# Told keys in three parts, x1 turned ahead of a fold piece, row places by when they come free, two more weight heads kept, 16-row bands

## The reference, cut to what matters

```python
def _peer_block(xb, wq, sub_keys, u_tab, v_tab):
    q = (xb @ wq).reshape(T, PEER_HEADS, 2, PEER_HALF)
    s = jnp.einsum('thpd,hpkd->thpk', q, sub_keys).astype(jnp.float32)
    s1, i1 = lax.top_k(s[:, :, 0], PEER_TOPK)          # 16 of 128
    s2, i2 = lax.top_k(s[:, :, 1], PEER_TOPK)
    cand = (s1[..., :, None] + s2[..., None, :]).reshape(T, PEER_HEADS, PEER_TOPK * PEER_TOPK)
    cidx = (i1[..., :, None] * PEER_KEYS + i2[..., None, :]).reshape(T, PEER_HEADS, PEER_TOPK * PEER_TOPK)
    top, sel = lax.top_k(cand, PEER_TOPK)              # 16 of 256
    idx = jnp.take_along_axis(cidx, sel, axis=-1)
    gate = jax.nn.softmax(top, axis=-1)
    h = jax.nn.gelu(jnp.einsum('td,thkd->thk', xb, u_tab[idx]).astype(jnp.float32), approximate=False)
    return jnp.einsum('thk,thkd->td', (gate * h).astype(xb.dtype), v_tab[idx])
# the pool mixer, per group g with window w in (2, 4, 8, 16): d = (mean of the last w rows of u) - u
```

## Time and profile before

| | |
|---|---|
| median of 3 runs | 3123.96 us |
| the profiled execution's own time | 3122.1 us |
| its span, first to last instruction | 3120.0 us |
| mean granted TensorE clock | 0.866 |
| busy: TensorE, VectorE, ScalarE, GpSimd | 74%, 71%, 31%, 43% |
| moved by the DMA engines | 1258.71 MB, mean 403 GB/s |

### The profile page before, as it was taken

One profiled execution on the slowest core, in us unless ns is written; L12 is line 12 of the kernel. 1 busy time (PEld: TensorE's weight loads), 2 busy tenths in 40 slices (PEclk: granted clock), 3 DMA queues, 4 the chain that ended last, 5 costly groups with the idle time before them and its releaser, 6 DMA issues.

```text
span 3120.0 us, 53529 instructions
## 1 busy us (share of the span) xinstructions
PE 2321.9 (74%) x21008; PEld 929.5 (30%) x21008; DVE 2219.2 (71%) x5418; ACT 954.4 (31%) x2437; POOL 1330.2 (43%) x1143
## 2 busy tenths in 40 slices
PE   8989998578777787668776667576677576767656
PEld 4633333233333333224432122122222122222112
DVE  1476777678878879656677666587777777777775
ACT  1422332334435435112322222132332332223222
POOL 1034344334444343345655544344444444444443
PEclk9999999889889899777878888798888898789867
DMA  7699999999999999999999999999999999999997
GB/s 282 238 420 421 420 402 419 417 419 384 419 418 409 418 409 404 415 406 418 416 418 412 417 413 398 418 414 420 409 415 403 420 419 421 402 420 419 420 416 309
DMA packets 201412, 1258.71 MB, mean 403 GB/s; under 512 B 24001, under 2 KB 27609, under 8 KB 60225
## 3 DMA queue, kind: packets, MB, share of 16 engines
q0 software_dynamic: 159808, 1133.76, 88.2%
q1 hardware_dynamic: 39916, 121.25, 10.0%
q10 hardware_dynamic: 1436, 0.29, 0.0%
HBM read 1226.74 MB, written 28.65 MB: 402 GB/s over the span
## 4 chain that ended last, share of the span: by engine, by line
DMA 31%; PE 14%; DVE 6%; POOL 4%; issue 3%; DVEq 2%; ACT 2%; POOLq 0%; ACTq 0%
DMA ring<-in_uv,idx 31%; PE sc L1044 7%; DVE ring L1929 3%; POOL ring L2151 3%; PE sc L1077 2%; PE route L1019 2%; DVEq L1939 1%; PE sc L1046 1%; ACT diag L1451 1%; POOL front L2167 1%; PE sc L943 0%; ACT hgelu L1446 0%; PE work L1065 0%; PE sc L913 0%; DVE x L1978 0%
## 5 line engine op out<-in xcount | busy, mean ns | idle before, releaser
L2151 POOL DMA_INDIRECT ring<-in_uv,idx x1056 | 1250.1, 1184 | 1617.5 <-PE sc L1046 1396.0
L1929 DVE CUSTOM_DVE_ANT_0 ring<-ring,xn_cur 128x1024 f32<-128x1024 f32 x1056 | 1280.8, 1222 | 649.2 <-DMA ring<-in_uv,idx 645.2
L1044 PE MATMUL sc<-ring,diag 32*32 32x512 f32 x8192 | 1229.1, 719 | 676.7 <-ACT diag L1451 631.6
L1046 PE MATMUL sc<-ring,diag 32*32 32x512 f32 x8192 | 1229.0, 719 | 0.0
L1044 PEld LDWEIGHTS sc<-ring,diag 32*32 32x32 f32 x8192 | 270.5, 117 | 1449.1 <-ACT diag L1451 1039.1
L1446 ACT ACTIVATE hgelu<-hdot 128x2 f32<-128x2 f32 x528 | 107.5, 204 | 1858.8 <-DVE hdot L1929 1857.9
L1451 ACT ACTIVATE diag<-gate_d,hgelu 128x32 f32<-128x32 f32 x1056 | 281.8, 314 | 21.2
L1046 PEld LDWEIGHTS sc<-ring,diag 32*32 32x32 f32 x8192 | 269.8, 117 | 1.9 <-issue 1.7
L589 PE MATMUL sc<-big,front 128*128 128x512 f32 x384 | 177.8, 606 | 2.2 <-DVE front L1558 2.1
L1446 ACT ACT_TABLE_LOAD x129 | 165.5, 1283 | 2.3
L1019 PE MATMUL route<-big,xnT 128*128 128x256 f32 x560 | 135.7, 397 | 0.0
(11 more groups left out here) (314 smaller groups left out, 2337.6 us busy)
## 6 DMA issues: line engine op xcount, KB each, us to landing
front<-wqk_scratch SPq DMA_DIRECT2D x21, 1024.0 KB, 13.0
ring<-in_uv,idx POOLq DMA_INDIRECT x1056
big<-in_w_in SPq DMA_DIRECT2D x8, 1024.0 KB, 13.8
wqk_scratch<-front SPq DMA_DIRECT2D x8, 1024.0 KB, 6.3
big<-wqk_scratch SPq DMA_DIRECT2D x8, 1024.0 KB, 22.2
x<-x_scratch SPq DMA_DIRECT2D x12, 512.0 KB, 9.0
ring<-in_wq_t POOLq DMA_DIRECT2D x10, 512.0 KB, 14.0
front<-in_x SPq DMA_DIRECT2D x8, 512.0 KB, 6.9
```

The lines of the kernel that those rows point to most:

```text
L1044: pe.matmul(sc[own, 0, :], diag[own, r, :], uv_rows[own, place, D:D + W4], start=opens_sum, stop=closes).then_inc(row_added[r], 1)
L1046: pe.matmul(sc[other, 1, :], diag[own, r, :], uv_rows[own, place, D + W4:2 * D], start=opens_sum, stop=closes).then_inc(row_added[r], 1)
L1929: dve.tensor_tensor_reduce(uv_rows[:, row_of(k), 0:D], uv_rows[:, row_of(k), 0:D], xn_cur[:, :], 1.0, 0.0, ALU.mult, ALU.add, hdot[:, n % ...
L2151: pool.indirect_dma_start(uv_rows[:, row_of(k), :], None, uv, bass.IndirectOffsetOnAxis(ap=idx[:, n % PH, j:j + 1], axis=0)).then_inc(row_ ...
```

## The change

First choice of keys (`choose_first`, `tell_keys`): for n = 0 alone, the index of the best expert is written as soon as the best 8 of each half are known, that of the next 7 after the best 8 sums, that of the last 8 after all; `fetch` waits for each part by itself. x1 of the first tile is turned before fold piece 14, which moves with piece 15 behind all four output products of tile 1; piece 14 comes to lie in `x2`, so that place 7 is free of it, and it is loaded two pieces earlier. The ring's places are taken in the order 5, 6, 7, 2, 3, 0, 1, 4. The product of the pooled half for both column halves of tile 1 now stands ahead of the heads' half. Heads 4 and 3 stay from n = 27 on: `STREAMED` is 27, the eight loads into `big` are reordered and four of them stand at slots 181, 182, 184 and 185, right behind the reads of the keys and values that they overwrite. Of u of the tile before and of its band only the last 16 rows are loaded and multiplied.

```diff
+BEFORE = PAD + 1
-STREAMED = 29
+STREAMED = 27
+STAYING = (4, 3, 2, 1, 0, 5, 6, 7)
 def fold_slot(j):
-    return -LEAD + (1, 2, 3, 4, 5, 6, 7, 8, 9, 10, 11, 12, 12, 13, 13, 15)[j]
+    return -LEAD + (1, 2, 3, 4, 5, 6, 7, 8, 9, 10, 11, 12, 12, 13, 16, 16)[j]
+def stay_slot(i):
+    if i < 2:
+        return ATT[-1].scores[H - 1][-1] + 1 + i
+    if i < H:
+        return ATT[-1].values[H - 1] - 1 + i
+    return BACK_FREE + i - H
 def pooled_slot(t, c):
-    return (POOLED_0[c], a.out[c])[t] if t < EARLY else a.norm[c]
+    return (POOLED_0[c], a.out[0])[t] if t < EARLY else a.norm[c]
-        FIRST_ROW = 5
+        ROWS = (5, 6, 7, 2, 3, 0, 1, 4)
-            return (k + FIRST_ROW) % RING
+            return ROWS[k % RING]
-            return (turned, other, xt[0], xt[1], xn_cur[:, :], turned, other, xn_cur[:, :])[j - PH]
+            return (turned, other, xt[0], xt[1], xn_cur[:, :], turned, x2[:, :], xn_cur[:, :])[j - PH]
-        WQ_AFTER = {12: 7, 13: 8, 14: 9, 15: 12}
+        WQ_AFTER = {12: 7, 13: 8, 15: 12}
+        FIRST_KEYS = (0, 1, TOPK // 2)
             def band(t):
-                        mm = pe.matmul(bank[w][:, cols], a.up[:, cols], a.bp[:, cols], start=False, stop=True)
+                        rows = slice(0, T if t < EARLY else BEFORE)
+                        mm = pe.matmul(bank[w][:, cols], a.up[rows, cols], a.bp[rows, cols], start=False, stop=True)
...
                 elif n < STREAMED:
                     pe.wait_ge(wst_in[head_of(n) % 2], 16 * streamed_to(n))
                 else:
-                    pe.wait_ge(wqk_in, 16 * PH)
+                    for h in range(COPIES * (n - N0), COPIES * (n - N0 + 1)) if n >= N0 else (head_of(n),):
+                        pe.wait_ge(big_in[STAYING.index(h)], 16 * 2)
...
-                if s == ROUTE_0 - 2:
-                    norm_root(0)
                 for j in range(FOLDS):
                     if s == fold_slot(j):
                         keep_fold(j)
+                        if j == FOLDS - 5:
+                            norm_root(0)
...
+            def tell_keys(at, told):
+                P = at.stop - at.start
+                over = lambda ap: ap.unsqueeze(1).to_broadcast([T, P, TOPK])
+                place = [cand[:, s * T:s * T + P * TOPK].rearrange("p (i j) -> p i j", i=P) for s in range(2)]
+                dve.drain()
+                dve.tensor_scalar(ab[:, 0, at], ind2[:, at], 4, None, ALU.logical_shift_right)
+                dve.tensor_scalar(ab[:, 1, at], ind2[:, at], 15, None, ALU.bitwise_and)
+                dve.drain()
+                dve.tensor_copy(abf[:, :, at], ab[:, :, at])
+                dve.drain()
+                for s in range(2):
+                    dve.tensor_tensor(place[s], abf[:, s, at].unsqueeze(2).to_broadcast([T, P, TOPK]), over(iota[:, :]),
+                                      ALU.is_equal)
+                dve.drain()
+                for s in range(2):
+                    dve.tensor_tensor(place[s], place[s], over(ind1f[:, s, :]), ALU.mult)
+                dve.drain()
+                for s in range(2):
+                    dve.tensor_reduce(pick[:, s, at], place[s], AX.X, ALU.add)
+                dve.drain()
+                dve.scalar_tensor_tensor(out=idx[:, 0, told], in0=pick[:, 0, told], scalar=float(NK),
+                                         in1=pick[:, 1, told], op0=ALU.mult, op1=ALU.add).then_inc(idx_ready, 1)
+            def choose_first():
+                take_scores(0)
+                first_keys(0)
+                dve.drain()
+                dve.tensor_copy(ind1f[:, :, 0:8], ind1[:, :, 0:8])
+                dve.drain()
+                dve.scalar_tensor_tensor(out=idx[:, 0, 0:1], in0=ind1f[:, 0, 0:1], scalar=float(NK),
+                                         in1=ind1f[:, 1, 0:1], op0=ALU.mult, op1=ALU.add).then_inc(idx_ready, 1)
+                other_keys(0)
+                first_pairs(0)
+                dve.tensor_copy(ind1f[:, :, 8:16], ind1[:, :, 8:16])
+                tell_keys(slice(0, 8), slice(1, 8))
+                dve.drain()
+                dve.max(top2[:, 8:16], cand_lo[:, :])
+                dve.tensor_scalar(gst[:, NTOP:NTOP + 1], top2[:, 0:1], -1.0, None, ALU.mult).then_inc(top_ready, 1)
+                dve.drain()
+                dve.max_index(ind2[:, 8:16], top2[:, 8:16], cand_lo[:, :])
+                tell_keys(slice(8, 16), slice(8, 16))
...
             def fetch(n, j):
                 k = n * TOPK + j
-                if j == 0:
-                    pool.wait_ge(idx_ready, n + 1)
-                if k == RING - FIRST_ROW:
+                if n == 0 and j in FIRST_KEYS:
+                    pool.wait_ge(idx_ready, FIRST_KEYS.index(j) + 1)
+                if n >= 1 and j == 0:
+                    pool.wait_ge(idx_ready, n + len(FIRST_KEYS))
+                if k == ROWS.index(2):
+                    pool.wait_ge(ready[S0], filled(S0, ("out", EARLY - 1, 0)))
+                if k == ROWS.index(0):
                     pool.wait_ge(ready[S1], filled(S1, ("out", EARLY - 1, 1)))
...
-                sp.dma_start(a.up, u_d[tile_rows(t - 1), :]).then_inc(att_in, 16)
+                sp.dma_start(a.up[0:BEFORE, :], u_d[t * T - BEFORE:t * T, :]).then_inc(att_in, 16)
...
-                sp.dma_start(by_group(a.bp), c_band_prev).then_inc(band_in, 16)
+                sp.dma_start(by_group(a.bp)[0:BEFORE], c_band_prev[T - BEFORE:T]).then_inc(band_in, 16)
...
-                for h in range(PH):
-                    if s == BACK_FREE + h:
-                        sp.wait_ge(ready[S1], filled(S1, ("out", NT - 1, 1)))
-                        sp.dma_start(wqk_sb[:, h, :], wqk_d[h]).then_inc(wqk_in, 16)
+                for i, h in enumerate(STAYING):
+                    if s == stay_slot(i):
+                        if i < 2:
+                            sp.wait_ge(ready[S1], filled(S1, ("scores", NT - 1, H - 1, 1)))
+                        elif i < H:
+                            sp.wait_ge(ready[WK], filled(WK, ("values", NT - 1)))
+                        else:
+                            sp.wait_ge(ready[S1], filled(S1, ("out", NT - 1, 1)))
+                        sp.dma_start(wqk_sb[:, i, :], wqk_d[h]).then_inc(big_in[i], 16)
```

More of the change, by code:

```diff
@@ L443, in front_and_experts @@
         stage_out = [sem(f"stage_out{i}") for i in range(2)]
-        w_in_in = [sem(f"w_in_in{k}") for k in range(KD)]
+        big_in = [sem(f"big_in{k}") for k in range(KD)]
         w_out_in = [sem(f"w_out_in_{n}") for n in ("heads", "pooled")]
@@ L486, in front_and_experts @@
         wst_in = [sem(f"wst_in{i}") for i in range(2)]
-        wqk_in = sem("wqk_in")
         gate_w_in = sem("gate_w_in")
@@ L570, in project_early @@
                 for k in range(KD):
-                    pe.wait_ge(w_in_in[k], 16)
+                    pe.wait_ge(big_in[k], 16)
                     for t in range(EARLY):
@@ L761, in front_step @@
                             out_pooled(t, c)
+                    for c in range(2):
                         if s == a.out[c]:
@@ L1011, in route @@
                             mm = pe.matmul(bank[RT][tokens, 0:256], xnT[:, k, tokens],
-                                           wqk_sb[:, head, k * 256:(k + 1) * 256],
+                                           wqk_sb[:, STAYING.index(head), k * 256:(k + 1) * 256],
                                            start=(k == 0), stop=(k == KD - 1))
@@ L1016, in route @@
                 else:
-                    w = wst[head_of(n) % 2] if n < STREAMED else wqk_sb[:, head_of(n), :]
+                    w = wst[head_of(n) % 2] if n < STREAMED else wqk_sb[:, STAYING.index(head_of(n)), :]
                     for k in range(KD):
@@ L1913, in join_keys @@
                                          in1=pick[:, 1, :], op0=ALU.mult, op1=ALU.add).then_inc(idx_ready, 1)
-            def choose(n):
-                take_scores(n)
-                first_keys(n)
-                other_keys(n)
-                first_pairs(n)
-                other_pairs(n)
-                split_pairs(n)
-                pick_keys(n)
-                join_keys(n)
+            def tell_keys(at, told):
[20 more added lines that the diff above has]
+                                         in1=pick[:, 1, told], op0=ALU.mult, op1=ALU.add).then_inc(idx_ready, 1)
@@ L2086, in _ @@
                 if s == ROUTE_0:
-                    choose(0)
+                    choose_first()
             dve.wait_ge(ready[A1], filled(A1, ("fold", FOLDS - 1)))
@@ L2122, in _ @@
         def _(pool):
-            pool.wait_ge(w_in_in[KD - 1], 16)
+            pool.wait_ge(big_in[KD - 1], 16)
             for i in range(2):
@@ L2132, in _ @@
                             pool.wait_ge(ready[b], filled(b, ("x", t)))
+                if j == FOLDS - 2:
+                    pool.wait_ge(ready[S1], filled(S1, ("scores", EARLY - 1, H - 1, 0)))
                 if j in WQ_AFTER:
@@ L2200, in load_w_in @@
             def load_w_in(k):
```

(10 more changed lines are left out.)

## The result

The changed kernel takes 3108.48 us in the median of 6 runs (3106.80 to 3113.12), the kernel before 3124.35 (6 runs, 3122.10 to 3126.84): a ratio of 0.9948, 95% interval 0.9939 to 0.9958. The forecast was 3106.0, its range 3098 to 3116. The profiled execution took 3106.8 us, its span is 3104.5, the mean granted clock 0.868.

A forecast was written before the change was run, and what follows sets the result against it. The loop was taken to be bound by bytes moved by the DMA. 6.4 + 5.0 + 2.0 + 4.7 = 18.1 us off the profiled 3122.1 gave 3104; the median standing 1.9 higher, 3106 us, range 3098 to 3116.

The forecast's parts named there:

- The lead: Loop's start, 138 to 150 us: earlier keys and gathers cut DMA idle time from 9.2 to 2.8 us, gain 6.4 us.
- The stretch behind it: After the first gathers: first dot product 1.3 to 2.3 us earlier, ninth gather about 4 us earlier, no new DMA gap.
- wrong if the ninth gather is not earlier than 163: Sign at the loop's start: the prediction is wrong if the ninth gather, before at 165.90, is not earlier than 163.
- Two streamed loads: Loads of n = 27 and 28 go, 2.10 MB at 418 GB/s: 5.0 us.
- The rival that the engines bound the stretch up to 1260: Attention, 700 to 1260, ends when its engines are done, whatever the DMA saves: gain 10.0, time 3114; chance 15%.
- Four loads moved: Four loads into `big` come between about 1165 and 1190, filling half the DMA's shortfall: 2 us, between 0 and 4.
- The bands: Attention, from near 525 up to 1110: ten transfers lose 112 of 128 rows, 2.29 MB; 85% taken, 4.7 us.
- the port rival: Band transfers: 16 rows load few paths that gathers share, so 2.7 us instead of 4.7, time 3108; chance 10%.
- The slower one: 1165 to 1200: the burst of four loads starves the engines, TensorE's clock falls to 1.2 GHz, time 3132; chance 4%.
- my second sign: Prediction is wrong if VectorE waits for rows more than 10 us in the last attention tile.
- The stalls: Rival: late rows and loads come sooner, the 1180 to 1260 shortfall and other dips give 4 more, 3100; chance 12%.
- The end of the attention: Sign: the attention ends 10 us or more earlier, with the rate after 1260 as before.

The follow-up runs named there:

- the run with the old order: Changed kernel with fold pieces 14 and 15 back at their old slots, keys still told in three parts: 3112.26 us, ratio 0.9961.
- the last experiment: Changed kernel with one head more kept, 26 as the first that stays: 3106.14 us, ratio 0.9940; again 3106.05 us, ratio 0.9935.
- the last table: Kernel without the computation, gathers beside loads of 2 KB rows with chosen partitions, seven stages: 1468.65 us; 128 rows 0.66 us, 16 adjoining 0.34 us a load.

## Why the prediction held, step by step

- *The lead, 6.4.* The keys and the first gathers were met closely: the choice starts at 136.99 (forecast 137.0), key 0 is told at 139.7 (139.7), the next seven at 145.4 (145.3), gathers 0 and 1 go out at 139.98 and 145.64 (140.0, 145.6), and 2.7 us idle time is left (2.8). That last agreement is partly luck, for the gap lies elsewhere: the forecast had the DMA dry from 144 to 146.8, and of the 2.7 us 1.6 lie before 142. SP's load for n = 2 went out at 139.38, not near 137, since it waited 2.4 us for the store issued at 132.26 to land. The share between 140 and 148 is 0.83, not near 0.5. What the experiments take away is 5.2 for the telling, and the reordering's share is in the same idle time; no run of the changed kernel took both away at once. By difference from the whole, 15.9 - 7.3 - 3.2, the lead is 5.4, 1 us under its term.
- *The stretch behind it* was mis-timed. The first dot product was to be 1.3 to 2.3 us earlier and is only 0.7 (157.72), and the ninth gather came at 165.06, not near 162. In the two other traces of the changed kernel both are earlier than before by 0.1 us alone. The cause stands in TensorE's and VectorE's timelines: both pieces end only at 155.3, VectorE waits 4.30 us for them before it lays the gates, and `route` for n = 1, for which TensorE waited 1.57 us on ScalarE's copy, takes 5.27 us where `route` for n = 0 took 3.67. The granted clock of 154 to 162 is 0.79, which is 3.4 of 8 us at its lower level, right after TensorE had been idle for 0.60 and 1.57 us. The ninth gather waits for the first sum behind it. The DMA had no new gap from it: the eight rows, the stores and the load for n = 2 kept its share at 0.98 from 150 to 154 and at 1.01 up to 170. The late load for n = 3 cost nothing either: it went out at 167.76, and `route` for n = 3 ran at 194.68 without a wait (forecast around 195). So the sign "wrong if the ninth gather is not earlier than 163" was a bad sign: the run with the old order has that gather at 162.72 and is slower.
- *Two streamed loads, 5.0.* Measured 4.5, and one more head 2.1 to 2.7 for its 2.5. The rival that the engines bound the stretch up to 1260 does not hold: n = 27's load, and with the last experiment n = 26's, paid like any others.
- *Four loads moved, 2.0.* Measured 2.7 by the medians and 1.6 by the means, within 0 to 4. The place was wrong: they went out at 1204 to 1226, not 1165 to 1190. The mechanism stands in the rates: the DMA's shares of 0.97 and 0.98 became 0.99 and 1.02. The prediction called all of 1180 to 1260 bound by the engines, but from 1210 to 1240 the DMA moved 419 GB/s before the change too.
- *The bands, 4.7.* This is the term that was most likely mis-sized. I priced ten transfers by their bytes, 0.55 us each, at 85%. By the last table each one saves 0.66 - 0.34 = 0.32 us, in all 3.2, with no discount for the engines. The kernel's own runs give the same 3.2 by the medians, but 4.4 by the means, so they alone would not rule out 4.7 or the port rival's 2.7; the price per transfer is what speaks for 3.2.
- *The rivals.* The slower one was to decide from about 11 us of waits in the last attention tile, and 10.8 came. But the granted clock was 1.00, 0.89 and 1.00 there, against 0.94, 0.94 and 1.00 before. With two levels, 1 and 0.5, that is 6.6 us at the lower one instead of 7.2, where the rival had 27 us of TensorE's work run at half speed. TensorE had work for 24.66, 23.54 and 17.19 us in these rows. VectorE waits there while the DMA's share is 0.99 to 1.02: the DMA is full and nobody is late; my second sign, over 10 us of waits, thus came true without the loss that I tied to it. The stalls did not shrink beyond the sum.
- *The end of the attention* was to be 10 us or more earlier, and this sign failed. SP's loads behind the last output product went out at 1265.61 instead of 1272.49, 6.9 us earlier (5.2 and 4.6 in the other two traces of the changed kernel), and the lead at the 385th gather was 7.9. It grew to 16.4 only behind that, where four loads into `big` and the one for n = 28 no longer stand. The rate after 1260 was as before, as forecast: 422 GB/s up to 1300 and 402 up to 1350 in both.
- *The sum.* 5.4 + 4.5 + 2.7 + 3.2 = 15.8, measured 15.9 (the lead in it is a difference, so this is no independent proof of it). The forecast of 18.1 was too high by 2.2: by the medians 1.5 are the bands, 1.0 the lead and 0.5 the streams, and the moved loads gave 0.7 back. Each of these is smaller than the scatter of its runs.

## What to carry to other kernels

Where the DMA engines bound a loop, price a change by the bytes that they fail to move: take their idle share before and after, and check each signal of the prediction (a first dot product, a wait) against that before calling it a sign of time. A wait for rows that appears where there was none can mean that the DMA is full there now, and need not be a loss. And price a narrow transfer by the partitions that it touches, not by its size.

## What the runs showed of the hardware that was not expected

- A load of 64 adjoining partitions (131 KB) took 0.81 us beside gathers (one run), more than one of 128 partitions and twice its bytes (0.66 us); the DMA rate fell from 414 to 324 GB/s. The DMA engines' share is 1.02 in both, so this share alone does not tell the one from the other.
- Landing takes long where the DMA is full. In the kernel before, the first five loads into `big`, 1 MB each, went out between 1272.5 and 1274.6 and landed 14.5, 20.0, 24.5, 29.0 and 33.4 us after their issue, 5 to 6 us one behind the other. A megabyte in 5 us is about half of the 422 GB/s that the DMA moved there; the gathers had the rest.
- Telling the choice in three parts costs VectorE 2.2 us: it begins 2.2 us earlier than before, and the last eight keys are told at the same time, 149.05 us against 149.04. Small operations of 0.15 to 0.5 us with a drain behind each are not free, though no gather waited for the last eight keys: gathers 8 and up had no free place before 165.
